# A sparse-attention and recurrence layer after its projection: pairs grouped around the compression inputs, and GpSimd's first rotation behind them

## What is computed

```python
def hybrid_layer(x, norm_g, w_in, ...):
    h = rms_norm(x, norm_g)
    proj = h @ w_in
    (q, kc, vc, ks, vs, kw, vw, gl, g_nsa, rwkv_in, g_rwkv) = _split(proj, IN_SIZES)
    o_nsa = nsa_mixer(q, kc, vc, ks, vs, kw, vw, gl,
                      cmp_pos_k, cmp_w1_k, cmp_w2_k, cmp_pos_v, cmp_w1_v, cmp_w2_v)
    o_nsa = o_nsa * jax.nn.silu(g_nsa.astype(jnp.float32))
    o_rwkv = rwkv7_mixer(rwkv_in, ...)
    o_rwkv = o_rwkv * jax.nn.silu(g_rwkv.astype(jnp.float32))
    mix = jnp.concatenate([o_nsa, o_rwkv], axis=-1).astype(x.dtype)
    return x + mix @ w_out

def compress_blocks(kv, pos_emb, w1, w2):
    B, G, S, D = kv.shape
    ch = kv.reshape(B, G, S // CMP_STRIDE, CMP_STRIDE, D)
    blk = jnp.concatenate([ch[:, :, :-1], ch[:, :, 1:]], axis=3) + pos_emb
    flat = blk.reshape(B, G, -1, CMP_BLOCK * D)
    return jax.nn.silu(flat @ w1) @ w2

def rwkv7_step(state, inp):
    r_t, w_t, k_t, v_t, kk_t, a_t = inp
    sa = jnp.einsum('bhvk,bhk->bhv', state, -kk_t)
    state = (state * w_t[:, :, None, :] + sa[..., None] * (kk_t * a_t)[:, :, None, :]
             + v_t[..., None] * k_t[:, :, None, :])
    y = jnp.einsum('bhvk,bhk->bhv', state, r_t)
    return state, y
```

## Time and profile before

| What | Value |
|---|---|
| Median of three runs | 1821.42 us |
| Lowest and highest | 1821.42 and 1822.37 us |
| Span of the profiled execution (its only time shown) | 1824.4 us |
| TensorE busy | 1745.1 us, 96% |
| VectorE, GpSimd, ScalarE busy | 933.1, 750.4, 536.9 us |
| Mean granted TensorE clock | 0.985 of 2.4 GHz |
| Bytes moved | 143.93 MB, mean 79 GB/s |

### The profile page before, as it was taken

The page is one execution under the profiler, slowest core; times in us unless marked ns, Lnnn a source line. Parts: engine busy times, 40 slices in busy tenths (PEclk is TensorE's granted clock), DMA queues, the critical chain, the costliest instruction groups (busy, mean ns, idle before and its releaser), DMA issues.

```text
span 1824.4 us, 28031 instructions
## 1 busy us (share of the span) xinstructions
PE 1745.1 (96%) x11622; PEld 1407.4 (77%) x11622; DVE 933.1 (51%) x1600; ACT 536.9 (29%) x1084; POOL 750.4 (41%) x375
## 2 busy tenths in 40 slices
PE   8999989999799989889999999999999999999999
PEld 5778767887667767677888888877876788888887
DVE  5676145667646356566656651234434366656311
ACT  3111133545324345544222220034222332222100
POOL 4343125300444122236555554462224565555542
PEclk9999998999899999999999999999999999999999
DMA  5222120000232321122333233231112233233232
GB/s 180 81 82 87 42 98 3 3 2 2 74 114 89 100 87 61 46 91 73 103 96 100 93 101 96 93 102 58 59 47 70 69 97 102 93 100 96 94 103 69
DMA packets 43644, 143.93 MB, mean 79 GB/s; under 512 B 5192, under 2 KB 7129, under 8 KB 43391
## 3 DMA queue, kind: packets, MB, share of 16 engines
q1 hardware_dynamic: 43518, 142.15, 24.2%
HBM read 139.50 MB, written 4.08 MB: 79 GB/s over the span
## 4 chain that ended last, share of the span: by engine, by line
PE 64%; DVE 4%; ACT 3%; issue 1%; POOL 1%; DVEq 0%; ACTq 0%; POOLq 0%
PE all_p_bank L206 19%; PE all_p_bank L208 19%; PE all_p_bank L207 19%; DVE l_sc L2565 1%; PE all_p_bank L2264 1%; PE all_p_bank L2240 1%; PE all_p_bank L2477 1%; DVE l_mx L2571 1%; PE all_p_bank L1991 0%; PE all_p_bank L2506 0%; PE all_p_bank L2948 0%; PE all_p_bank L2930 0%; POOL b_wlo L187 0%; PE all_p_bank L2943 0%; PE all_p_bank L2251 0%
## 5 line engine op out<-in xcount | busy, mean ns | idle before, releaser
L187 POOL TENSOR_TENSOR b_wlo<-b_raw,b_whi 128x1024 fp32r<-128x1024 f32 x238 | 580.2, 2441 | 764.7 <-DVE b_whi L180 761.2
L206 PE MATMUL all_p_bank<-b_hi,b_whi 128*128 128x512 f32 x1248 | 508.6, 407 | 10.3 <-issue 6.1
L208 PE MATMUL all_p_bank<-b_hi,b_wlo 128*128 128x512 f32 x1248 | 490.5, 393 | 0.0
L207 PE MATMUL all_p_bank<-b_lo,b_whi 128*128 128x512 f32 x1248 | 490.0, 393 | 0.0
L180 DVE CAST b_whi<-b_raw 128x1024 fp32r<-128x1024 f32 x238 | 187.0, 792 | 443.7 <-PE all_p_bank L208 426.6
L206 PEld LDWEIGHTS all_p_bank<-b_hi,b_whi 128*128 128x128 f32 x1248 | 236.8, 190 | 78.2 <-issue 25.4
L207 PEld LDWEIGHTS all_p_bank<-b_lo,b_whi 128*128 128x128 f32 x1248 | 237.2, 190 | 51.1 <-issue 5.1
L208 PEld LDWEIGHTS all_p_bank<-b_hi,b_wlo 128*128 128x128 f32 x1248 | 236.6, 190 | 50.9
L206 PE MATMUL all_p_bank<-f_mhi,b_whi 128*128 128x512 f32 x352 | 136.9, 389 | 0.0
L207 PE MATMUL all_p_bank<-f_mlo,b_whi 128*128 128x512 f32 x352 | 136.9, 389 | 0.0
L208 PE MATMUL all_p_bank<-f_mhi,b_wlo 128*128 128x512 f32 x352 | 136.9, 389 | 0.0
(11 more groups left out here) (465 smaller groups left out, 2590.0 us busy)
## 6 DMA issues: line engine op xcount, KB each, us to landing
b_raw<-in_w_up SPq DMA_DIRECT2D x88, 512.0 KB, 3.5
b_raw<-in_w_down SPq DMA_DIRECT2D x44, 512.0 KB, 3.4
b_raw<-in_w_in SPq DMA_DIRECT2D x32, 512.0 KB, 3.5
b_raw<-in_w_out SPq DMA_DIRECT2D x24, 512.0 KB, 3.5
b_raw<-in_w_gla SPq DMA_DIRECT2D x22, 512.0 KB, 3.5
b_raw<-in_w_diff SPq DMA_DIRECT2D x20, 512.0 KB, 3.5
b_raw<-in_w_mem SPq DMA_DIRECT2D x8, 512.0 KB, 3.5
all_x<-in_x SPq DMA_DIRECT2D x8, 256.0 KB, 5.5
```

The source lines that it names most:

```text
L187: self.nc.gpsimd.tensor_tensor(self.lo[:, n % SLOTS, :], self.raw[:, n % RAWS, :], self.hi[:, n % SLOTS, :].bitcast(F32), ALU.subtract).th ...
L206: nc.tensor.matmul(acc, lhsT=left[0], rhs=right[0], start=first, stop=False)
L207: nc.tensor.matmul(acc, lhsT=left[0], rhs=right[1], start=False, stop=False)
L208: return nc.tensor.matmul(acc, lhsT=left[1], rhs=right[0], start=False, stop=last)
```

## The change

In the plan `second`, the first seven ticks are written out: pair, inputs, pair, pair, inputs, pair, pair. The remaining 8 steps of `Recurrent` and 9 of `Sparse` up to the keys are spread evenly as before, and so come in another phase. From the keys on the plan is the same. In `Sparse.rotate`, GpSimd's first rotation waits for `s_xp` to be 8 (all eight additions of the inputs) in place of `projected`.

```diff
@@ Sparse.rotate
         if n == 0:
-            pool.wait_ge(*self.projected)
+            pool.wait_ge(self.s_xp, 8)
             pool.wait_ge(self.i_cos, 16)
@@ first_layer
-    second = spread(split - chunks, keys) + spread(tail - split, sparse.n - keys)
+    second = [1, 0, 1, 1, 0, 1, 1] + spread(split - chunks - 5, keys - 2)
+    second += spread(tail - split, sparse.n - keys)
```

## The result

The changed kernel takes 1826.7 us in the median of ten executions (1822.53 to 1830.56), the kernel before 1822.3 in as many (1821.42 to 1827.2). The ratio is 1.0022, with an interval of 1.0012 to 1.0031: slower by about 4 us. The forecast was 1823.6, with a range that ended at 1825.4. The ratio weighs all executions and lies near the ratio of the means, so it need not be that of the two medians.

A forecast was written before the change was run, and what follows sets the result against it. TensorE, busy 96% of the span, was taken as the bound, so only its idle or lower-clock time counted. Keys +0.6 plus a second clock fall +1.6 gave +2.2; 1821.42 + 2.2 = 1823.6 us, range 1819.2 to 1825.4.

The forecast's parts named there:

- The first gap: TensorE's idle time before the first hidden step: inputs ready later, step +0.4 us; pairs 2 to 4 moved in, 3.83 saved.
- The clock in the first gap: Around the first hidden step: clock falls and returns as before, at about 238.8; step again 3.6 us, rope +0.6.
- the second rival: First gap: clock stays up, hidden step saves 1.7 us, rope 0.5; 1819.9, or 1821.5 with the second fall; chance 0.14.
- The stall at the gates: Before L852: TensorE waits for ScalarE's copy of turn 8, table load and sigmoid, 2.7 us.
- The 0.49 us before L867: Before the keys: nothing covers ScalarE's silu after the lift; keys at 257.45 against 256.86, +0.6 us by the sum.
- The fall behind the stall: Behind the gates' wait: clock falls for 3.4 us, losing 1.6 us, so +2.2 us at the keys.
- the rival without a fall: Behind the gates' wait: clock doesn't fall, work on both sides being dense; +0.6, 1822.0 us; chance 0.18.
- The step that failed: From the keys to the end: same order on every engine, so the +2.2 us shift is passed on.
- The sign that the prediction set itself: Forecast is wrong if, among others, the stretch from the keys (L867) to the end isn't as long as before.
- The base: Whole kernel: +2.2 us from a profile of span 1824.4 was added to the median of 1821.42, giving 1823.6.
- The third: Behind the gates' wait: the lower clock lasts twice as long, twice 1.6 us lost; +3.8, 1825.2 us; chance 0.13.
- The fifth: Later, such as behind 284.89: the shift moves a clock fall away; 1.6 us less, 1820.4 to 1822; chance 0.10.

The follow-up runs named there:

- the wait alone: Kernel before, with only GpSimd's first rotation waiting for all eight additions: 1824.89 us, ratio 1.0009.
- the stall filled: Changed kernel with 13 throwaway identity products on TensorE ahead of the gates' transposes, while it waits for the sigmoid: 1821.07 us, ratio 0.9992.
- sigmoid early: Changed kernel with ScalarE's sigmoid and silu of the gates put back to the projection's end, ahead of turn 8's copy: 1822.34 us, ratio 0.9984.
- tail kept: Changed kernel's first seven ticks and GpSimd wait, then the tick order of before (gates ahead of turn 8, lift ahead of turn 11): 1819.76 us, ratio 0.9981.
- later or all gaps filled: Changed kernel with identity products: 9 and 12 in the two gaps before L1392, 1823.18 us; or 11 at the gates, 7 and 9 there, 1822.16 us.
- control: The kernel before, run again unchanged: 1821.58 us (1820.6 to 1827.12), ratio 0.9998.

## Why the prediction was wrong, point by point

**The first gap: right.** +0.4 was forecast for the hidden step, +0.6 measured (8.64 against 8.04). The parts show: VectorE's additions at 0.67 us each, the 0.94 us of the wait (7.10 against 8.04 with the wait alone; 0.95 forecast), and pairs 2 to 4 in the gap for nothing.

**The clock in the first gap: varies.** It was forecast to fall as before. It stayed up in the changed kernel's profile, as the second rival had it, and in that of the kernel with the stall filled. It fell in the other four profiles with the same order and wait up to there and no filler in this gap: sigmoid early, tail kept, and the changed kernel with the later or all gaps filled. In the changed kernel's profile this is why the keys stand at +0.1 and not at +2.2: the second rival put the hidden step and the rope at 2.2 us less.

**The stall at the gates: right in place, cause and size.** 2.64 us against 2.7, made of the parts that were named. The Trainium skill (ScalarE: Activation LUTs, § What ACT_TABLE_LOAD costs) gives 1283 ns for the load and adds a drain, 2.66 us in all. The rows agree with the first, 1.28 us, and not with the sum: the sigmoid starts 0.01 us behind the load. The 0.49 us before L867 are there too.

**The fall behind the stall: right in size, but not always there.** It came in the changed kernel's profile (0.89 from 245 to 260) and cost the 1.6 us that were forecast: from the gates' transposes to the keys it took 8.06 us, against 6.43 where the same stall had no fall behind it. The prediction read that in its own trace the clock is down at the latest 1.3 us after TensorE resumes; behind the gap before 284.89 it is down only after 1.7. And for the rival without a fall it named the 1.88 us before 598.88, but not the 1.87 us before 276.18 in the same trace, which have a fall right behind them. That row showed that the length of the idle time doesn't decide. What was missed is what goes along with this fall: filling the stall took away 5.6 us in the median.

**The step that failed** is the sentence behind it: "From there on both kernels have the same order on every engine, and what follows hangs on TensorE or on chains that start from it; the shift is passed on." The order is the same, the time isn't: of the 6.0 us between the changed profile and the control's, 4.9 arise between the scores and the first unit, by falls of the clock at the scores and the two gaps before L1392. The sign that the prediction set itself says so too: from the keys to the last product the changed kernel takes 1566.28 us, the kernel before 1564.33 in the prediction's profile and 1560.92 in the control's. Filling only those two gaps took 3.5 us off the changed kernel and made the two kernels level.

**The base was wrong with it.** The sum was made against a profile in which the later falls are present (span 1824.4), and then carried over to a median of 1821.42 in which, as the control shows, they mostly aren't. The text noted the 3.0 us between the two and asked no further. About that much was the term that it put at nothing: 3.3 us is what the stretch from the first level to the first unit gains where the clock stays up (16.51 against 13.26). The forecast in the profile's measure, 1824.4 + 2.2 = 1826.6, looks like the measured median of 1826.7, but it is a span, and the span that goes with 1826.69 is 1824.7. From the projection's end the two profiles do lie 2.06 us apart, near the 2.2. That is luck: the keys were at +0.1, and a fall at the scores that wasn't in the sum brought 1.6 us more.

**The rivals.** The third, the one for slower, was placed behind the new stall, with a doubled fall. Slower it was, but the extra falls came 13 and more us later. The fifth had only a later fall that goes away, on the ground that the profile had them; that the changed kernel could meet them in most executions where before did in a third wasn't among the rivals, and could not be with a profile taken as the rule.

**What stays open.** Why one execution has the falls and another of the same kernel hasn't isn't visible in any row: the idle time ahead is the same 1.88 us, or 2.64 at the gates. That the share of executions with falls changes with a shift of 0.9 us in the front (the wait alone, nine of eleven against a third) is measured, its rule isn't. Nor is it shown for single executions that the fall behind the stall causes the later ones; it is shown that filling the stall takes most of the long executions away. A rival to that is left: every filler also moves what follows, by 0.4 us at the gates, and neither a filler that keeps TensorE busy without moving anything nor a shift of the same 0.4 us without one was run. Most executions weren't profiled, so how many of the changed kernel's meet the later falls is inferred from their times and mean clocks. What would keep the clock up in the scores wasn't tried.

## What to carry to other kernels

When a tick plan is shifted, look at each engine's queue for the instruction that was early for free: here a sigmoid with its table load had lain 23 us ahead of its reader, and one tick put it behind turn 8's copy, where it held up the gates' transposes. Where TensorE has idle stretches of about 2 us, a single profile is one draw of which of them lower the clock: take the profile's span against the median of several executions, and where they differ by more than the effect to be forecast, find out which falls make the difference before anything is added to either. And the price of idle time on TensorE isn't its length: with the wait at the gates filled with throwaway products the changed kernel was level with before, and with the same wait left empty its median was 5.6 us higher.

## What wasn't expected of the hardware

- The same idle time, 1.88 us before the same instruction, is followed by a fall of the granted clock in one execution and not in another (0.78 against 1.00 from 272 to 295). The two falls of that stretch together cost 2.9 to 3.3 us between the first level and the first unit in the five profiles that have them. The same holds for the stall of 2.64 us at the gates: 8.06 us to the keys with a fall, 6.43 without.
- The clock also fell where TensorE was busy throughout, in and behind products of 31 columns: 0.72 from 260 to 272 with 12.00 us busy of 12. In the control it stayed at 1.00 in the same products.
- A kernel's executions then lie in two groups 5 us apart. The mean granted clock tells them: 0.987 to 0.989 and 0.983 to 0.985 in the control.
- A product of two 128 x 128 tiles of this kind takes 0.23 to 0.24 us in a row of them (3.17 us for 13), and with 7 and 9 of them in the gaps of 1.9 us the clock was at 1.00 from 272 to 295 in all four profiles; without fillers it was there in three of eight.
